# Weight splits of the way out moved from the end of the projections into the levels of the last inverses

## The reference

```python
h = rms_norm_2(x, a_norm1_g[i])
proj = h @ a_w_in[i]                       # ain0 .. ain5
...                                        # token shift, decay, rates, gate
y = rwkv7_scan(rh, decay, kh, vh, -kk, kk * lrh)
y = head_group_norm(y, a_lnx_g[i], a_lnx_b[i])
y = y + sum(rh * kh * a_r_k[i]) * vh
m = memory_attention(q_mem, mem_n, a_mem_kv[i])
x = x + concatenate([y * gate, m]) @ a_w_out[i]    # aout0, aout1: "the way out"
x = x + swiglu_2(rms_norm_2(x, a_norm2_g[i]), a_ffn_gu[i], a_ffn_down[i])   # ff1
```

## Time and profile before

| | |
|---|---|
| median of 3 runs | 1306.73 us |
| the profiled execution, its own time | 1301.55 us |
| its span, first to last instruction | 1300.2 us |
| busy: PE, DVE, ACT, POOL | 92%, 60%, 44%, 5% of the span |
| mean granted clock of TensorE | 0.956 of full speed |
| low parts (L1230), high parts (L1909) | 164 each, 374.7 and 312.6 us busy |

### The profile page before, as it was taken

One profiled execution on the slowest core, in us unless ns is written; L12 is line 12 of the kernel. 1 busy time (PEld: TensorE's weight loads), 2 busy tenths in 40 slices (PEclk: granted clock), 3 DMA queues, 4 the chain that ended last, 5 costly groups with the idle time before them and its releaser, 6 DMA issues.

```text
span 1300.2 us, 21981 instructions
## 1 busy us (share of the span) xinstructions
PE 1192.7 (92%) x9627; PEld 1102.9 (85%) x9627; DVE 774.0 (60%) x964; ACT 572.5 (44%) x750; POOL 69.6 (5%) x132
## 2 busy tenths in 40 slices
PE   5998889899999999897789799999988889999998
PEld 5776679689999999894678699999986769999997
DVE  4455766546655557685784466555584666655553
ACT  4353455345434445234312644344463555434443
POOL 2310020000100000200000010000011000100000
PEclk8998999999999999897799899999988999999999
DMA  5952334333455456340000055555542403455551
GB/s 202 325 157 93 128 132 160 130 121 139 164 193 192 177 185 217 117 179 29 1 3 3 14 175 182 195 179 181 191 167 92 162 1 130 165 193 194 181 179 63
DMA packets 29947, 185.00 MB, mean 142 GB/s; under 512 B 3547, under 2 KB 6816, under 8 KB 8860
## 3 DMA queue, kind: packets, MB, share of 16 engines
q1 hardware_dynamic: 24176, 174.07, 37.4%
q0 software_dynamic: 2464, 7.11, 1.9%
q10 hardware_dynamic: 3212, 2.42, 0.6%
HBM read 180.18 MB, written 3.41 MB: 141 GB/s over the span
## 4 chain that ended last, share of the span: by engine, by line
PE 75%; DVE 12%; ACT 7%; issue 3%; POOL 2%; DMA 1%; ACTq 0%; DVEq 0%; POOLq 0%
PE bank L603 72%; DVE w_lo L1230 2%; DVE inverse_rms_rows L1322 2%; ACT w_hi L1909 2%; PE bank L725 1%; PE bank L752 1%; DVE stats L1387 1%; ACT exps L1998 1%; DMA w_raw<-in_weights 1%; DVE logits L1379 1%; POOL channel_inverse_rms L2331 1%; ACT x_channels_hi L1959 0%; POOL inverse_rms_diagonals L2322 0%; PE bank L619 0%; DVE inverse L1806 0%
## 5 line engine op out<-in xcount | busy, mean ns | idle before, releaser
L1230 DVE TENSOR_TENSOR w_lo<-w_raw,w_hi 128x2048 fp32r<-128x2048 f32 x164 | 374.7, 2291 | 241.9 <-ACT w_hi L1909 241.8
L1909 ACT ACTIVATE w_hi<-w_raw 128x2048 fp32r<-128x2048 f32 x164 | 312.6, 1913 | 152.0 <-DMA w_raw<-in_weights 149.0
L603 PE MATMUL bank<-x_channels_hi,w_hi 128*128 128x256 f32 x1232 | 200.1, 285 | 1.1 <-DVE w_lo L1230 1.1
L603 PE MATMUL bank<-x_channels_lo,w_hi 128*128 128x256 f32 x1232 | 198.4, 284 | 0.0
L603 PE MATMUL bank<-x_channels_hi,w_lo 128*128 128x256 f32 x1232 | 191.0, 277 | 0.0
L603 PEld LDWEIGHTS bank<-x_channels_hi,w_hi 128*128 128x128 f32 x1232 | 171.4, 194 | 1.4 <-DVE w_lo L1230 1.2
L603 PEld LDWEIGHTS bank<-x_channels_lo,w_hi 128*128 128x128 f32 x1232 | 168.3, 191 | 0.1
L603 PEld LDWEIGHTS bank<-x_channels_hi,w_lo 128*128 128x128 f32 x1232 | 165.9, 190 | 0.0
L603 PE MATMUL bank<-hidden_hi,w_hi 128*128 128x256 f32 x528 | 106.4, 283 | 0.0
L603 PE MATMUL bank<-hidden_lo,w_hi 128*128 128x256 f32 x528 | 106.2, 283 | 0.0
L603 PE MATMUL bank<-hidden_hi,w_lo 128*128 128x256 f32 x528 | 103.2, 277 | 0.0
(11 more groups left out here) (425 smaller groups left out, 1723.1 us busy)
## 6 DMA issues: line engine op xcount, KB each, us to landing
w_raw<-in_weights SPq DMA_DIRECT2D x164, 1024.0 KB, 4.8
bias_rows<-bias_lines POOLq DMA_DIRECT2D x3, 768.0 KB, 6.1
mem_rows<-in_mem POOLq DMA_DIRECT2D x2, 1024.0 KB, 5.3
bias<-bias_rows ACTq DMA_DIRECT2D x1, 1536.0 KB, 14.0
xn<-in_x SPq DMA_DIRECT2D x1, 1024.0 KB, 4.9
out<-xn SPq DMA_DIRECT2D x2, 512.0 KB, 3.1
wide_masks<-in_triangle_masks POOLq DMA_DIRECT2D x1, 832.0 KB, 8.2
bias<-bias_rows ACTq DMA_DIRECT2D x1, 768.0 KB, 7.4
```

The lines of the kernel that those rows point to most:

```text
L603: return nc.tensor.matmul(out, lhs, rhs, start=start, stop=stop)
L1230: V.tensor_tensor(k.w_lo[:, s, :], k.w_raw[:, s, :], k.w_hi[:, s, :].bitcast(F32), ALU.subtract).then_inc(k.lo_done, 1)
L1909: A.activation(k.w_hi[:, s, :], k.w_raw[:, s, :], ACT.Copy).then_inc(k.hi_done, 1)
```

## The change

A new piece `unit` stands in the order, in levels 2 to 5 of the last inverses, behind the first `beside` piece and ahead of `second`. ScalarE makes there the high part and VectorE the low part of one unit of the way out: U in level 2, U+1 in level 3, U+2 in level 4, U+3 in level 5. TensorE, POOL and SP have no share in it. To keep these units for it, `hi` and `lo` stop at a bound, `split["end"]`, which is U up to the end of the projections; it is lifted to the whole stream as the recurrence begins. What `product` asks for beyond the bound is then dropped, and what it asks for behind the recurrence, for units already split, does nothing. `recurrence_vector` and `recurrence_scalar` are handed `lo` and `hi` for it.

```diff
@@ recurrence_order
     for level in range(1, LEVELS + 1):
         order += [("first", 2, level), ("first", 3, level), beside.pop(0) + (0,)]
+        order += [("unit", level - 2, 0)] if level > 1 else []
         order += [("second", 2, level), ("second", 3, level), beside.pop(0) + (0,)]
@@ vector_program
-    split = {"n": 0}
+    split = {"n": 0, "end": k.of["aout0"][0][0]}
     def lo(n):
-        while split["n"] < min(n, k.total_units):
+        while split["n"] < min(n, split["end"]):
...
-    recurrence_vector(k, attention)
+    split["end"] = k.total_units
+    recurrence_vector(k, attention, lo)
@@ recurrence_vector
             V.tensor_tensor(k.state[:, n + 1, :, :], bank[6][:, 0:RWB * C].rearrange("p (b v) -> p b v", b=RWB),
                             k.state_factor[:, :, n:n + 1].to_broadcast((P, RWB, C)), ALU.mult).then_inc(k.st_v.sem, 1)
+        elif piece == "unit":
+            lo(k.of["aout0"][0][0] + n + 1)
         elif piece in ("rhs", "u") and n >= 2:
@@ scalar_program
-    split = {"n": 0}
+    split = {"n": 0, "end": k.of["aout0"][0][0]}
     def hi(n):
-        while split["n"] < min(n, k.total_units):
+        while split["n"] < min(n, split["end"]):
...
-    recurrence_scalar(k, attention)
+    split["end"] = k.total_units
+    recurrence_scalar(k, attention, hi)
@@ recurrence_scalar
+        elif piece == "unit":
+            hi(k.of["aout0"][0][0] + n + 1)
         elif piece == "y":
             A.wait_ge(*k.y_p.at("chunk", n))
```

More of the change, by code:

```diff
@@ L1681, in raw_channels, with recurrence_vector @@
                                    in1=k.raw[:, b, 1:S + 1], op0=ALU.mult, op1=ALU.add).then_inc(k.dve_once.sem, 1)
-def recurrence_vector(k, attention):
+def recurrence_vector(k, attention, lo):
     nc, V, bank, sh = k.nc, k.nc.vector, k.bank, k.sh
@@ L2213, in scalar_program, with recurrence_scalar @@
                      scale=k.rstd_cols("last")[:, 1:2]).then_inc(k.last_rows_a.sem, 1)
-def recurrence_scalar(k, attention):
+def recurrence_scalar(k, attention, hi):
     A, bank, sh = k.nc.scalar, k.bank, k.sh
```

## The result

| | before | changed |
|---|---|---|
| median of 20 runs each | 1306.11 us | 1315.12 us |
| lowest to highest | 1301.74 to 1316.48 | 1309.16 to 1329.46 |
| the profiled execution's span | 1300.2 us | 1314.2 us |
| mean granted clock | 0.956 | 0.946 |

The ratio of the times is 1.0062, with a 95% interval of 1.0041 to 1.0083: 8.1 us, or 5.4 to 10.8. Forecast were 1313.1 us, in a range of 1309.0 to 1317.5. The lines of the code from 578 on moved by one to seven; L1231 and L1913 are now the low and the high part, L604 is the matmul, L1831 the add, L1808 the turn, L1888 the copy of rhs 2.

A forecast was written before the change was run, and what follows sets the result against it. TensorE's order of work was taken to set the end at all three places. Old places 0 + 0, levels 5.6 and clock 0.8 made 6.4 us, added to 1306.73 for 1313.1 us; range 1309.0 to 1317.5.

The forecast's parts named there:

- The old places: Ahead of and behind the recurrence: removing the splits gives back 0; bounds 2.3 us per low part ahead, 4.5 us behind.
- The rival of a late load at the front: At the projections' end: U+1's load usually lands later, so removing splits there makes it faster, 1304.0 us; chance 0.05.
- The levels: Last inverses, levels 2 to 5: splits there cost 0.4, 3.45, 0.25 and 1.45 us, sum 5.6.
- the order of ScalarE's own list: Levels 3 and 5: high part waits behind u 1's second copy or the memory copy; costs 3.45 and 1.45 us.
- behind u 2 every piece hangs on TensorE's order: From u 2 to the end: the levels' shift of 5.6 us goes through whole.
- the 5 to 7 that were named as a sign: Way out: TensorE begins aout0 5 to 7 us later than 739.22.
- 711.3 to 712: End of level 5: u 2 starts near this time, after TensorE waits about 2 us for the rhs copy.
- The clock: Levels 4 and 5: TensorE's waits bring one fall of the granted clock, costing 0.8 us; none gives 0, two full 3.4.
- The rule of the Trainium skill: Gaps ahead of level 4 and u 2: both paid in full at half rate, sum 9.0 instead of 6.4 us.
- No change, the levels hide the splits: Levels 3 and 5: high parts ready in time, low parts cost 0.25 to 0.5 us each, 1308.2 us; chance 0.08.
- Worse: Clock falls at both gaps and stays low into the chunks behind u 2, adding 10.7 us, 1317.4 us; chance 0.2.

The follow-up runs named there:

- e1: Changed kernel, but only the first 16 of 2048 columns of the way out's four units are split, output left wrong; ratio to before 1.0002 (0.9984 to 1.0021).
- e2: Changed kernel with ScalarE making all four high parts in one go between first and last inverses, low parts left in levels 2 to 5; ratio to before 1.0048.
- e3: Changed kernel with only aout0's two units split beside levels 2 and 3, aout1's behind the recurrence as before; ratio to before 1.0045.
- e4: Changed kernel with only aout1's two units split beside levels 4 and 5, aout0's ahead of the recurrence as before; ratio to before 1.0027.
- e5: Changed kernel with TensorE's 2.1 us wait ahead of u 2 filled by 16 transposes of a constant; ratio to before 1.0012 (0.9986 to 1.0037).
- e6: Kernel with high parts between first and last inverses and low parts beside the four variance pieces; ratio to before 0.9959, run again 1.0013.
- e8: Kernel before with 90 instead of 30 transposes ahead of aout0 and 5 more ahead of u 2; ratio to before 0.9998 (0.9971 to 1.0025).

## Why the prediction was right

**The old places.** Priced at 0, measured at 0: e1's ratio is 1.0002, and the two engines' waits grew by what they were relieved of. The interval of that ratio ends 2.1 us under before; the stretches at both places bound it closer. The rival of a late load at the front had nothing to stand on; ScalarE's idle 1.01 us and VectorE's 0.27 were small but real, and TensorE had none.

**The levels.** Taken from u 0, before at 677.96 and changed at 682.54, a shift of 4.58 us that is older than the levels, the extra delay is

| at | before | changed | extra | forecast |
|---|---|---|---|---|
| u 1, behind level 2 | 687.08 | 692.10 | 0.44 | 0.4 |
| state 1, behind level 3's turns | 692.88 | 701.34 | 3.88 | 3.85 |
| memory, behind level 4's turns | 700.24 | 708.94 | 4.12 | 4.1 |
| u 2 | 705.73 | 715.98 | 5.67 | 5.6 |

The step that decided was the order of ScalarE's own list: in levels 3 and 5 the high part stood behind a copy that waits for TensorE, and the low part, the adds, the turns and the copy of rhs 2 all stood in line behind it. e2 takes only that away and 4.45 us are gone. That a loss is not caught up by later levels was right too (e3, e4). One reading behind them was not: "behind u 2 every piece hangs on TensorE's order". Between the rows shown of the chain of waits it leaves TensorE at 719.54 for the copy of u 3 and, but for 0.93 us at 726.01, stays on ScalarE and VectorE until 739.22. Ahead of aout0 TensorE waits 7.53 us:

```profile
739.22 1.20 PE L603 MATMUL bank<-amix_channels_hi,w_hi 128*128 128x256 f32 x4 [7.53 <-ACT amix_channels_hi L2294]
```

The shift went through whole all the same, since that part of the chain starts from TensorE's u 3, but the extra 0.36 us of e5's paragraph arise there. So aout0 begins 7.4 us later than before once the 4.3 that are older are taken off, a little outside the 5 to 7 that were named as a sign; u 2, 4.58 us taken off, begins at 711.40, inside its 711.3 to 712.

**The clock.** This term was misplaced and a little too small. I added 0.8 us for a fall in levels 4 and 5, where the wait of about 3 us lies. There was none: granted clock in windows of the changed kernel (us, busy and instructions by engine, clock, DMA):

```profile
696.00:700.00 4.00, 0.98 (x26) 0.84 (x25) 3.92 (x5) 2.29 (x2) 0.00 (x0) 1.00 0.00 0
700.00:711.00 11.00, 10.83 (x262) 9.51 (x259) 8.15 (x12) 1.86 (x3) 0.00 (x0) 1.00 0.01 3
716.00:721.00 5.00, 5.00 (x28) 3.75 (x28) 0.66 (x2) 1.09 (x3) 0.00 (x0) 0.50 0.00 0
```

and before, behind its u 2:

```profile
707.00:711.00 4.00, 4.00 (x32) 2.25 (x32) 1.12 (x2) 1.93 (x3) 0.00 (x0) 0.57 0.00 0
```

The wait of 3.02 us lies in the first window, the levels behind it in the second, both at full clock. The fall came at u 2 instead, and as the clock fell behind u 2 before as well, only what it lasted longer is the change's: 1.11 us, which e5 gives back. With the 0.36 us of VectorE's that is the 1.47 by which the chunks are longer (34.96 against 33.49). So the recurrence loses 5.67 + 1.11 + 0.36 = 7.1 us, and 0.28 in the front that is older, against 5.6 + 0.8 = 6.4 forecast. That the 0.8 came so near is luck: it was worked out for another place, and the fall that the kernel before already had was not seen, since the window of the earlier trace rows ends at 703. The rule of the Trainium skill, "TensorE: Matmul & The Clock Gate", section "HAM oscillation — how this bites in real kernels", that idle stretches between bursts send the array to half rate, would, as the prediction applied it, have had both waits paid, 9.0 us in all. Its own example has longer waits, for a DMA, so it does not speak of waits like these; here the measurement decides: the array fell to 1.2 GHz in the 2.13 us ahead of u 2 (0.55 over 715 to 716) and stayed at 2.4 GHz behind the 3.02 us of level 4.

**The whole.** The time moved by 8.1 us (5.4 to 10.8), and the trace puts 7.1 into the recurrence. "No change, the levels hide the splits" is what e6 makes of the kernel, and e2 nearly, and not what the changed order does. "Worse" named a mechanism that does exist, at one of its three places.

## What to carry to other kernels

Ask of every piece of work that is to be moved what it stands in the way of at its old place: if the engine only waits for the bound engine behind it, there is nothing to give back. At the new place count the queue twice, once for the piece itself and once for the piece on another engine that it needs, with everything that engine has to do first. If two engines share a piece, the first half can go early, to an idle stretch, and the second half into a wait that is longer than it is.

## What was not expected of the hardware

TensorE idled 3.02 us ahead of level 4 and kept its full clock (1.00 over 696 to 711), and yet was at half by u 2, behind a wait of 2.13 us. Before the change it went through u 2 at full clock and fell in the centring behind it (1.00 over 706 to 707, 0.61 over 707 to 708), 1.5 us behind a wait of only 0.57 us. Five transposes of 0.77 us in all, in the place of that short wait, kept the clock at 1.00 for the next 10 us (e8). What sets these cases apart is open. And the same instructions in stages far from the change ran at a mean clock of 0.93 in one execution and 1.00 in another, which moves the whole by nearly as much as the change does (3.2 us from 166 to 240, 2.5 after 1026).
